# The first norm moved into the inputs' stage, with two queue and engine moves in the projection and the compressor

## The chip, the cores and the metric

The kernel runs on one core of one Trainium2 chip. A core has five engines that run side by side, each in its own program order: TensorE (PE, matrix products), VectorE (DVE), ScalarE (ACT), GpSimd (POOL) and SyncE (SP, which here only issues transfers). Semaphores tie them together; 16 DMA engines move data. The time is device microseconds (us) of one execution, the median of several.

## The reference

One step of a decoder layer in float32: 1024 prompt tokens and 8 x 4 sample tokens of width 1024. The input is normalised per token, scaled and shifted by two vectors of adaLN, and projected; beside attention over compressed, selected and window keys runs an S5 state-space branch; an MLP closes the layer. What the change touches:

```python
def rms_norm(x, g):
    y = x * lax.rsqrt(jnp.mean(x * x, axis=-1, keepdims=True) + RMS_EPS)
    return y * g

def mixer_inputs(x, c, lw):
    mods = ada_mods(c, lw['w_ada'], lw['b_ada'])          # silu(c) @ w_ada + b_ada, in 6 parts
    h = rms_norm(x, lw['g_norm_mix']) * (1 + mods[1]) + mods[0]
    proj = jnp.einsum('ntd,de->nte', h, lw['w_in'])
    ...

def compress(x, pe, w1, b1, w2):                          # cached keys and values, in chunks of 16 tokens
    ...
    part = jnp.einsum('ncsgd,jsde->jncge', x, w1c)
    hid = b1 + jnp.einsum('jsd,jsde->e', pec, w1c)
    for j in range(CMP_RATIO):
        hid = hid + part[j, :, j:j + n_cmp]
    return jnp.einsum('ncge,ef->ncgf', jax.nn.silu(hid), w2)
```

## The kernel before

The kernel is a row of stages: inputs, norm, SSM, projection, compressor, prompt attention, decode attention, tail. Each opens its own buffers and semaphores and closes with a barrier of all engines. Within a stage each engine has its own hand-written program.

**Inputs** (`stage_inputs`, L95). SP loads the nine blocks of rows of x (`xrow`: eight of 128 prompt tokens, one of 32 sample tokens), then the four blocks of adaLN weights (`wada`, two buffers: block i+2 waits until the products of block i are done), then `wu`, the SSM's columns of the input weights. PE turns each block of rows (L177) so that channels lie on partitions; DVE copies the even blocks from PSUM to `xT`, ACT the odd ones, two halves of four channel groups each (L129). Then PE makes the adaLN products (L86) block by block, DVE copies them, PE sums them per channel (L92), and DVE adds the bias: `mod`.

**Norm** (`stage_norm`, L221). SP stores `xT` to DRAM (`x_keep`, for the tail; L258). On `xT`, in three slices of 352 tokens by 8 channel groups, ACT squares (L282), PE sums over channels with a matrix of ones (L303), ACT takes the root, DVE inverts and multiplies, and ACT scales and shifts by `amp` and `mod` (L272) into `hT`. The sample tokens, which have their own vectors, get two more DVE operations per channel group.

**SSM** (`stage_ssm`, L378). PE begins with the products of `hT` and `wu` (L549); SP begins with the loads of the SSM's parameters, which PE turns after the first 16 products (L528). The buffers of this stage lie where `xT` was.

**Projection** (`stage_project`, L1066, with `table_steps`, L933). PE multiplies `hT` by the input weights, block after block of 128 columns (x = 0, 1, ...; two weight buffers, `w_raw`). SP issues each block's weights when the products of block x-2 are done, and all else in program order between them: at x == 3 it issues the store `bias_lines` (`store_line`: eight rows of 383, each written 128 times, to DRAM) and at x == 5 the copies of the two window caches from DRAM to DRAM. ACT rounds the weights (`weights_hi`, L1186) and copies PE's sums from PSUM (L1201 to L1207), in this order:

```python
                    ins.then_inc(kept, 1)
                    if s == 0 and 1 <= x < NX - 1:
                        weights_hi(x + 1)
                if x == 1:
                    t_near_bias(act)
```

**Compressor** (`stage_compress`, L1251). There are 18 units: i = 0 and 1 are the prompt's keys and values, the other 16 the keys and values of the eight sequences' caches. POOL gathers the pages of a unit by two indirect transfers of 128 x 2048 (`raw`, two buffers). They are then regrouped by key head into `byg`, one half by DVE (L1455), the other by ACT (L1400). PE turns a unit in eight turns of four transposes (L1336); ACT rounds each turn to `x_hi` (L1382), DVE makes the remainder `x_lo` (L1426), and PE multiplies: eight steps (sp) of three products. Unit i+1 is turned between the steps of unit i. The sums go to `hid` by DVE (L1433) and ACT (L1394); after step 6 PE makes the second products (L1313, L1319) of the unit before. The order of turns and steps on PE:

```python
                    if i + 1 < NI and NH[i + 1] == 2 and sp >= 1:
                        turn(i + 1, sp - 1)
                        if sp == 7:
                            turn(i + 1, sp)
                    if sp == 6 and i >= 1:
                        second(i - 1)
```

## Time and profile before

| | us |
|---|---|
| median of 3 runs | 2280.38 (2274.66 to 2280.99) |
| the profiled execution | 2283.11 |
| its span in the trace | 2281.1 |
| inputs, from 0 to | 47.62 |
| norm, to | 83.3 |
| SSM, to | 298.4 |
| projection, to | 467.5 |
| compressor, to | 681.8 |
| attention of prompt and decode, to | 1104 |
| tail, to | 2281.1 |

The trace has one row for each instruction or for a run of like ones: start, duration, engine, line, what is written and read; in brackets how long the engine had idled and what ended that. A name with a q (SPq) is the engine's sequencer, which issues transfers. PE is busy for 91% of the span, in the tail nearly throughout; the holes lie in the stages before it. Over the span the page gives PE's granted clock in 40 slices, mostly at 0.9 and over.

### The profile page before, as it was taken

The numbers are of one execution on the slowest core, as the hardware profiler recorded it, in microseconds if no ns is written. First come the engines' busy times: TensorE is split into PE (matmuls) and PEld (weight loads), VectorE is DVE, ScalarE is ACT, GpSimd is POOL, SyncE is SP. The second block draws the span as 40 slices with busy tenths as digits, with TensorE's granted clock in tenths as the row PEclk, the third lists the DMA queues.
The fourth block names the chain that finished last, engine by engine and source line by source line (L and its number), as shares of the span: only waits on it lengthen the run. The fifth ranks groups of instructions, "written<-read, shape, count | busy, mean of one in ns | idle before, by whom it ended". The sixth has DMA issues, their size and how long they took to land.

```text
span 2281.1 us, 33862 instructions
## 1 busy us (share of the span) xinstructions
PE 2069.8 (91%) x13956; PEld 1860.0 (82%) x13956; DVE 913.3 (40%) x1739; ACT 805.0 (35%) x1603; POOL 532.6 (23%) x478
## 2 busy tenths in 40 slices
PE   6694988969989999967799999999999999999997
PEld 4463678957775677745799999999999999999997
DVE  1568031126654777537411114454214313313424
ACT  2421321136654777734422223233113203302313
POOL 0190000011106656322122221121212222211220
PEclk8897889979996999979899999999999999999999
DMA  8102135354523321186611113111111111111111
GB/s 333 26 1 40 79 66 146 81 166 185 188 75 92 89 79 55 38 306 264 218 47 47 40 44 123 38 38 47 47 47 47 47 47 38 47 47 47 47 56 77
DMA packets 219065, 201.98 MB, mean 89 GB/s; under 512 B 37374, under 2 KB 202214, under 8 KB 210256
## 3 DMA queue, kind: packets, MB, share of 16 engines
q1 hardware_dynamic: 207118, 131.82, 19.9%
q0 software_dynamic: 9216, 67.11, 7.8%
q8 instruction: 111, 1.82, 0.3%
q10 hardware_dynamic: 2578, 0.88, 0.2%
q14 instruction: 42, 0.34, 0.0%
HBM read 178.05 MB, written 21.58 MB: 88 GB/s over the span
## 4 chain that ended last, share of the span: by engine, by line
PE 49%; DMA 1%; DVE 0%; ACT 0%; SPq 0%; issue 0%; ACTq 0%; DVEq 0%
PE ps L2286 16%; PE ps L2284 16%; PE ps L2285 16%; PE ps L2430 1%; DMA tail<-in_w_in 1%; DMA tail<-x_keep 1%; PE ps L2451 0%; DVE tail L2795 0%; ACT tail L2624 0%; DVE tail L2771 0%; SPq L2396 0%; SPq L2409 0%; ACT tail L2615 0%; DVE tail L2713 0%; ACT tail L2529 0%
## 5 line engine op out<-in xcount | busy, mean ns | idle before, releaser
L2284 PE MATMUL ps<-tail,tail 128*128 128x356 f32 (+2 forms) x2304 | 757.1, 329 | 12.0 <-POOL tail L2682 9.4
L2286 PE MATMUL ps<-tail,tail 128*128 128x356 f32 (+2 forms) x2304 | 750.7, 326 | 0.0
L2285 PE MATMUL ps<-tail,tail 128*128 128x356 f32 (+2 forms) x2304 | 748.7, 325 | 0.0
L2682 POOL TENSOR_TENSOR tail<-tail,tail 128x1024 fp32r<-128x1024 f32 x96 | 232.4, 2420 | 926.6 <-ACT tail L2529 926.6
L2284 PEld LDWEIGHTS ps<-tail,tail 128*128 128x128 f32 x2304 | 435.8, 189 | 15.1 <-POOL tail L2682 9.6
L2285 PEld LDWEIGHTS ps<-tail,tail 128*128 128x128 f32 x2304 | 435.8, 189 | 2.6 <-issue 0.2
L2286 PEld LDWEIGHTS ps<-tail,tail 128*128 128x128 f32 x2304 | 435.9, 189 | 0.0
L2529 ACT ACTIVATE tail<-tail 128x1024 fp32r<-128x1024 f32 x96 | 101.0, 1052 | 322.8 <-PE ps L2286 314.3
L2713 DVE SCALAR_TENSOR_TENSOR tail<-ps,mod,tail 128x346 f32<-128x346 f32 (+2 forms) x120 | 68.7, 572 | 345.8 <-PE ps L2286 336.4
L1746 POOL TENSOR_SCALAR pr<-pr,row_reciprocals,gT 128x640 f32<-128x640 f32 (+7 forms) x128 | 98.7, 781 | 112.8 <-DVE row_reciprocals L1865 111.2
L2584 ACT ACTIVATE tail<-tail,tail 128x346 f32<-128x346 f32 (+2 forms) x96 | 55.9, 583 | 195.5 <-DVE tail L2753 100.2
L1426 DVE TENSOR_TENSOR x_lo<-ps,x_hi 128x512 fp32r<-128x512 f32 (+1 forms) x136 | 89.0, 673 | 79.8 <-ACT x_hi L1382 78.7
L2696 DVE TENSOR_TENSOR tail<-tail,tail 128x346 f32<-128x346 f32 (+2 forms) x48 | 28.9, 601 | 210.0 <-ACT tail L2549 210.0
L2747 DVE TENSOR_TENSOR tail<-ps,tail 128x346 f32<-128x346 f32 (+2 forms) x96 | 50.3, 524 | 154.2 <-PE ps L2286 95.2
L1382 ACT ACTIVATE x_hi<-ps 128x512 fp32r<-128x512 f32 (+1 forms) x136 | 75.8, 580 | 79.0 <-PE ps L1336 78.7
L1657 PE MATMUL ps<-consts,pr 128*128 128x128 f32 (+7 forms) x592 | 93.5, 284 | 8.2 <-POOL pr L1746 6.4
L2284 PE MATMUL ps<-h_lo,w_hi 128*128 128x352 f32 x264 | 88.8, 336 | 9.2 <-DVE w_lo L1218 9.2
L1336 PE MATMUL ps<-consts,byg 128*128 128x128 f32 (+1 forms) x544 | 80.4, 279 | 18.4 <-DMA byg<-out 18.4
L1809 ACT ACTIVATE pr<-ps,nmax 128x640 f32<-128x640 f32 (+7 forms) x128 | 90.0, 703 | 19.1 <-DVE nmax L1845 16.3
L1336 PEld LDWEIGHTS ps<-consts,byg 128*128 128x128 f32 (+1 forms) x544 | 67.0, 147 | 33.2 <-DMA byg<-out 18.9
L1845 DVE TENSOR_REDUCE nmax<-ps 128x1 f32<-128x640 f32 (+7 forms) x128 | 90.6, 708 | 4.4
L2285 PE MATMUL ps<-h_hi,w_lo 128*128 128x352 f32 x264 | 88.0, 334 | 0.0
(481 smaller groups left out, 3024.2 us busy)
## 6 DMA issues: line engine op xcount, KB each, us to landing
tail<-in_w_ff SPq DMA_DIRECT2D x64, 512.0 KB
wada_late<-in_w_ada SPq DMA_DIRECT2D x32, 512.0 KB, 4.0
wada<-in_w_ada SPq DMA_DIRECT2D x4, 2048.0 KB, 12.2
tail<-in_w_in SPq DMA_DIRECT2D x16, 512.0 KB
x_keep<-xT SPq DMA_DIRECT2D x1, 4224.0 KB, 11.5
h_keep<-hT SPq DMA_DIRECT2D x1, 4224.0 KB
tail<-x_keep SPq DMA_DIRECT2D x1, 4224.0 KB, 13.1
xrow<-in_x_prompt SPq DMA_DIRECT2D x8, 512.0 KB, 8.2
```

What stands on the lines that cost most here:

```text
L1336: mm = pe.transpose(bank[y % 4][:, o:o + m], byg[0:m, i % 2, half, g, s:s + 2, :].rearrange("p s d -> p (s d)"), e.ident[0:m, 0:m])
L1382: act.activation(to, src, ACT.Copy).then_inc(hi_kept, 1)
L1426: dve.tensor_tensor(to, src, move(i, b, xhi)[1], ALU.subtract).then_inc(lo_kept, 1)
L1657: mm = pe.transpose(b[0:n, (t % 4) * P:(t % 4 + 1) * P], pr[:, u % NPR, t * n:(t + 1) * n], e.ident)
L1746: pool.tensor_scalar(p, p, rinv[:, k:k + 1], gT[:, qb, h:h + 1], ALU.mult, ALU.mult).then_inc(scaled, 1)
L1809: act.activation(p, score(s), ACT.Exp, bias=nmax[:, s % 4:s % 4 + 1], accum_out=rsum[:, sum_at(s):sum_at(s) + 1]).then_inc(exps_done, 1)
L1845: dve.tensor_reduce(nmax[:, u % 4:u % 4 + 1], s, AXX, ALU.max, negate=True).then_inc(maxima_done, 1)
L2284: pe.matmul(out, whi[:, kw, :], xlo(kx), start=(i == 0), stop=False)
L2285: pe.matmul(out, wlo[:, kw, :], xhi(kx), start=False, stop=False)
L2286: mm = pe.matmul(out, whi[:, kw, :], xhi(kx), start=False, stop=(i == n - 1))
L2529: act.activation(whi[:, x % 2], wraw[:, x % 2], ACT.Copy).then_inc(w_hi, 1)
L2682: pool.tensor_tensor(wlo[:, x % 2], wraw[:, x % 2], whi[:, x % 2], ALU.subtract).then_inc(w_split, 1)
```

## The change

Three stages are edited.

**Inputs and norm.** `stage_norm` is gone. In `stage_inputs` ACT squares the rows of x as they arrive, with the sum of each row taken in the same instruction (`ssq`), and takes the root of all nine columns at once; DVE inverts it (`rstd`). DVE copies all turned blocks to `xT`. The rows are then scaled in place by `rstd`, the odd blocks by ACT, the even ones by DVE, and PE turns the scaled rows a second time (`turn_scaled`), three blocks ahead of each of the weight blocks 1, 2 and 3. ACT copies the first halves of these turns to `hT`, DVE the second halves. When `mod` is there, `hT` is scaled and shifted in place: the prompt tokens of four channel groups by ACT, of four by DVE, and the sample tokens by two DVE instructions. SP issues the store of `x_keep` behind `wu`. It isn't waited for in this stage: in the SSM ACT waits for it ahead of its copies to `UT`, and DVE ahead of `Fre` and `Fim`; these three buffers are now allocated last.

**Projection.** `bias_lines` is issued by ACT at the end of x == 1, the window copies by ACT at the end of x == 5; SP issues neither.

**Compressor.** POOL regroups both halves, and issues the gathers of unit i+2 behind the regrouping of unit i. Ahead of its first gathers it waits for the prompt's rows. PE makes two turns after each odd step.

```diff
@@ stage_inputs
+            sp.wait_ge(x_kept, 2 * TB + 2)
+            sp.dma_start(e.x_keep, e.xT[:, :, :]).then_inc(e.x_stored, 16)
...
+            act.wait_ge(sums_set, 1)
+            for tb in range(TB + 1):
+                n = tokens(tb)
+                load_wait(act, x_loaded[tb], 1)
...
+                act.activation(junk[0:n, tb % TB, :], xrow[0:n, tb, :], ACT.Square, accum_out=ssq[0:n, tb:tb + 1]).then_inc(squared, 1)
...
+            act.activation(rstd[:, :], ssq[:, :], ACT.Sqrt, bias=e.eps, scale=1.0 / D).then_inc(root, 1)
+            act.wait_ge(rstd_set, 1)
             for tb in range(1, TB + 1, 2):
-                copy_x(act, tb)
+                act.wait_ge(x_turned, 2 * tb + 2)
+                act.activation(xrow[:, tb, :], xrow[:, tb, :], ACT.Copy, scale=rstd[:, tb:tb + 1]).then_inc(rows_act, 1)
+            for tb in range(TB + 1):
+                act.wait_ge(h_turned, 2 * tb + 1)
+                out, src = turned_to(e.hT, tb, 0)
+                act.activation(out, src, ACT.Copy).then_inc(h_kept[0], 1)
+            act.wait_ge(amp_set, 2)
+            act.wait_ge(h_kept[0], TB + 1)
+            for k in range(KD // 2):
+                act.activation(e.hT[:, k, 0:T], e.hT[:, k, 0:T], ACT.Identity, bias=e.mod[:, k, 0:1], scale=amp[:, k, 0:1]).then_inc(modulated, 1)
...
+            def turn_scaled(tb):
+                n = tokens(tb)
+                pe.wait_ge((rows_dve, rows_act)[tb % 2], tb // 2 + 1)
+                for h in range(2):
+                    if tb >= 2:
+                        pe.wait_ge(h_kept[h], tb - 1)
+                    else:
+                        pe.wait_ge(x_kept, 2 * TB + 2)
+                    for k in range(4):
...
+                    mm.then_inc(h_turned, 1)
+
             for i in range(NBLK):
+                if i:
+                    for tb in range(3 * (i - 1), 3 * i):
+                        turn_scaled(tb)
                 load_wait(pe, w_loaded[i % 2], i // 2 + 1)
...
+            for tb in range(TB + 1):
+                for h in range(2):
+                    dve.wait_ge(x_turned, 2 * tb + h + 1)
+                    dve.tensor_copy(*turned_to(e.xT, tb, h)).then_inc(x_kept, 1)
+            dve.wait_ge(root, 1)
+            dve.reciprocal(rstd[:, :], rstd[:, :]).then_inc(rstd_set, 1)
+            dve.wait_ge(rstd_set, 1)
             for tb in range(0, TB + 1, 2):
-                copy_x(dve, tb)
+                n = tokens(tb)
+                dve.tensor_scalar(xrow[0:n, tb, :], xrow[0:n, tb, :], rstd[0:n, tb:tb + 1], None, ALU.mult).then_inc(rows_dve, 1)
             for i in range(NBLK):
+                if i:
+                    for tb in range(3 * (i - 1), 3 * i):
+                        dve.wait_ge(h_turned, 2 * tb + 2)
+                        dve.tensor_copy(*turned_to(e.hT, tb, 1)).then_inc(h_kept[1], 1)
...
+            dve.tensor_scalar(amp[:, :, :], e.mod[:, KD:2 * KD, :], 1.0, None, ALU.add).then_inc(amp_set, 1)
...
+            for k in range(KD // 2, KD):
+                dve.tensor_scalar(e.hT[:, k, 0:T], e.hT[:, k, 0:T], amp[:, k, 0:1], e.mod[:, k, 0:1], ALU.mult, ALU.add).then_inc(modulated, 1)
...
+            dve.tensor_tensor(by_sequence, by_sequence, each(amp[:, :, 1:NC9]), ALU.mult).then_inc(samples, 1)
+            dve.wait_ge(samples, 1)
+            dve.tensor_tensor(by_sequence, by_sequence, each(e.mod[:, 0:KD, 1:NC9]), ALU.add).then_inc(samples, 1)
...
-def stage_norm(nc, e, tag, src, gain, shift=None, scale=None, dst=None, keep=None, store=False):
...
@@ stage_ssm
+            load_wait(act, e.x_stored, 1)
             for b in range(U_FIRST):
                 keep_turned(b)
...
+            load_wait(dve, e.x_stored, 1)
             for l, m in ((0, 4), (4, 4), (8, 1)):
...
@@ stage_project
-                if x == 3:
-                    t_store_line(sp)
...
-                if x == 5:
-                    for o, b in ((e.s_k_win, e.cache_k_win), (e.s_v_win, e.cache_v_win)):
...
                 if x == 1:
                     t_near_bias(act)
+                    t_store_line(act)
+                if x == 5:
+                    for o, b in ((e.s_k_win, e.cache_k_win), (e.s_v_win, e.cache_v_win)):
...
@@ stage_compress
+            for i in range(2):
+                load_wait(pool, prompt_rows_landed[i], 2)
+            gather(2)
+            gather(3)
+            for i in range(2, NI):
+                load_wait(pool, pages_landed[i % 2], 2 * (i // 2))
+                pool.wait_ge(turned, first[i - 1])
+                for half in range(2):
+                    dst, src = regrouping(i, half)
+                    pool.tensor_copy(dst, src).then_inc(regrouped, 1)
+                if i + 2 < NI:
+                    gather(i + 2)
...
-                    if i + 1 < NI and NH[i + 1] == 2 and sp >= 1:
+                    if i + 1 < NI and NH[i + 1] == 2 and sp % 2 == 1:
                         turn(i + 1, sp - 1)
-                        if sp == 7:
-                            turn(i + 1, sp)
+                        turn(i + 1, sp)
```

Where instructions stand: PE in the inputs' stage, before. The rows with `xrow` are the turns, those with `wada` the adaLN products (eight to a block), those with `modrow` their sums:

```order
L177 MATMUL ps<-consts,xrow 128x128 x64
L177 MATMUL ps<-consts,xrow 128x32 x8
L86 MATMUL ps<-wada,scT 32x512 x16
L92 MATMUL ps<-consts,modrow 128x9 x4
L86 MATMUL ps<-wada,scT 32x512 x8
L92 MATMUL ps<-consts,modrow 128x9 x4
L86 MATMUL ps<-wada,scT 32x512 x8
L92 MATMUL ps<-consts,modrow 128x9 x8
```

The same engine and stage in the changed kernel:

```order
L204 MATMUL ps<-consts,xrow 128x128 x64
L204 MATMUL ps<-consts,xrow 128x32 x8
L86 MATMUL ps<-wada,scT 32x512 x8
L227 MATMUL ps<-consts,xrow 128x128 x24
L86 MATMUL ps<-wada,scT 32x512 x8
L92 MATMUL ps<-consts,modrow 128x9 x4
L227 MATMUL ps<-consts,xrow 128x128 x24
L86 MATMUL ps<-wada,scT 32x512 x8
L92 MATMUL ps<-consts,modrow 128x9 x4
L227 MATMUL ps<-consts,xrow 128x128 x16
L227 MATMUL ps<-consts,xrow 128x32 x8
L86 MATMUL ps<-wada,scT 32x512 x8
```

The second turns (L227) stand in threes of blocks ahead of the weight blocks 1, 2 and 3.

SP in the projection, before, from the store at x == 3 on (`out<-rows` stores the new key and value rows):

```order
L969 DMA bias_lines<-line 8x128x383
L1113 DMA w_raw<-in_w_in 128x8x128
L1123 DMA out<-rows 128x8x128
L1125 DMA out<-rows 32x128
L1113 DMA w_raw<-in_w_in 128x8x128
L1123 DMA out<-rows 128x8x128
L1125 DMA out<-rows 32x128
L1131 DMA out<-in_cache_k_win 8x4x16256
L1131 DMA out<-in_cache_v_win 8x4x16256
L1110 DMA w_raw<-in_w_in 128x8x64 x2
```

The same place in the changed kernel:

```order
L1032 DMA w_raw<-in_w_in 128x8x128 x3
L1040 DMA out<-rows 128x8x128
L1042 DMA out<-rows 32x128
L1032 DMA w_raw<-in_w_in 128x8x128
L1040 DMA out<-rows 128x8x128
L1042 DMA out<-rows 32x128
L1029 DMA w_raw<-in_w_in 128x8x64 x2
```

`bias_lines` and the window copies have left this queue; the weights follow each other with only the row stores between.

ACT in the compressor, one unit before:

```order
L1382 ACTIVATE x_hi<-ps 128x4x128 x4
L1400 ACTIVATE byg<-raw 128x16x2x64
L1394 ACTIVATE hid<-hid,cbias 64x2x255
L1382 ACTIVATE x_hi<-ps 128x4x128 x4
L1389 ACTIVATE low<-ps 64x512
```

One unit and the next one's first rows in the changed kernel:

```order
L1310 ACTIVATE x_hi<-ps 128x4x128 x4
L1322 ACTIVATE hid<-hid,cbias 64x2x255
L1310 ACTIVATE x_hi<-ps 128x4x128 x4
L1317 ACTIVATE low<-ps 64x512
L1310 ACTIVATE x_hi<-ps 128x4x128 x4
```

The regrouping that stood ahead of `hid` is gone from ACT (and likewise from DVE); on POOL two of them stand between the gathers.

## Rows read from the trace of the kernel before

**Rows 1.** Norm, projection, compressor: length, each engine's busy time (instructions), PE clock, DMA.

```profile
47.60:83.30 35.70, 16.33 (x48) 9.83 (x48) 21.46 (x45) 29.18 (x60) 0.00 (x0) 0.74 0.29 122
298.40:467.50 169.10, 152.60 (x950) 149.66 (x950) 33.61 (x41) 33.50 (x49) 5.77 (x18) 0.92 0.41 99
467.50:681.80 214.30, 179.66 (x1080) 148.46 (x1080) 125.76 (x192) 126.86 (x190) 32.05 (x32) 0.92 0.46 162
```

**Rows 2.** Timeline of inputs and norm, PE and SP: start, duration, instruction, [idle before].

```profile
9.93 9.73 PE L177 MATMUL ps<-consts,xrow 128*128 128x128 f32 x72
...
27.03 3.19 PE L86 MATMUL ps<-wada,scT 128*32 128x512 f32 x16 [4.09 <-DMA wada<-in_w_ada]
...
32.01 1.92 PE L86 MATMUL ps<-wada,scT 128*32 128x512 f32 x16 [0.42 <-DMA wada<-in_w_ada]
...
39.19 3.64 PE L86 MATMUL ps<-wada,scT 128*32 128x512 f32 x16 [4.27 <-DMA wada<-in_w_ada]
...
47.62 0.35 SPq L258 DMA_DIRECT2D x_keep<-xT  x1
...
83.36 9.91 PE L549 MATMUL ps<-wu,hT 128*128 128x512 f32 x16 [18.38 <-PEq L66]
```

**Rows 3.** Groups by line, forms apart: count, busy us, mean ns, idle before.

```profile
L2615 ACT ACTIVATE tail<-tail,tail 128x1024 f32<-128x1024 f32 x4 | 4.5, 1147 | 0.7 <-DVE tail L2782 0.7
...
L2788 DVE TENSOR_SCALAR tail<-tail,tail 128x1024 f32<-128x1024 f32 x4 | 2.9, 751 | 0.1
...
L129 DVE COPY xT<-ps 128x512 f32<-128x512 f32 x8 | 5.2, 687 | 3.6 <-PE ps L177 3.6
```

**Rows 4.** DMA issues on the page: count, KB, us from issue to landing.

```profile
x_keep<-xT SPq DMA_DIRECT2D x1, 4224.0 KB, 11.5
```

**Rows 5.** Timeline of the projection, SP's issues and ACT.

```profile
333.73 0.31 SPq L969 DMA_DIRECT2D bias_lines<-line  x1
351.88 0.38 SPq L1113 DMA_DIRECT2D w_raw<-in_w_in  x1
...
357.31 0.46 ACT L1207 ACTIVATE turn_in<-ps 128x352 f32<-128x352 f32 x1 [4.96 <-PE ps L2286]
369.69 1.06 ACT L1186 ACTIVATE w_hi<-w_raw 128x1024 fp32r<-128x1024 f32 x1 [11.91 <-DMA w_raw<-in_w_in]
...
378.23 0.46 ACT L1207 ACTIVATE turn_in<-ps 128x352 f32<-128x352 f32 x1 [6.78 <-PE ps L2286]
...
391.44 0.47 ACT L1207 ACTIVATE turn_in<-ps 128x352 f32<-128x352 f32 x1 [5.04 <-PE ps L2286]
```

**Rows 6.** Timeline of the compressor: a second product of PE, DVE's last sums.

```profile
558.92 1.10 PE L1319 MATMUL ps<-w2c,hid 64*128 64x64 f32 x8 [0.84 <-ACT hid L1394]
...
640.08 0.67 DVE L1433 TENSOR_TENSOR hid<-ps,low 64x510 f32<-64x510 f32 x1
...
651.27 0.67 DVE L1433 TENSOR_TENSOR hid<-ps,low 64x510 f32<-64x510 f32 x1
...
662.02 0.67 DVE L1433 TENSOR_TENSOR hid<-ps,low 64x510 f32<-64x510 f32 x1
...
672.28 0.67 DVE L1433 TENSOR_TENSOR hid<-ps,low 64x510 f32<-64x510 f32 x1
```

**Rows 7.** Timeline of the compressor's start, PE's turns.

```profile
488.02 0.69 PE L1336 MATMUL ps<-consts,byg 64*128 64x64 f32 x4 [7.59 <-DMA byg<-out]
...
496.24 1.08 PE L1336 MATMUL ps<-consts,byg 128*128 128x128 f32 x4
```

**Rows 8.** POOL: two groups by line, then two rows of the SSM's timeline.

```profile
L1148 POOL COPY vslc<-rows 128x512 f32<-128x512 f32 x2 | 1.2, 614 | 54.1 <-DVE rows L1245 54.1
...
L2682 POOL TENSOR_TENSOR tail<-tail,tail 128x1024 fp32r<-128x1024 f32 x96 | 232.4, 2420 | 926.6 <-ACT tail L2529 926.6
...
141.03 1.17 POOL L517 TENSOR_TENSOR w<-w 128x16 f32<-128x16 f32 x1
...
150.72 0.21 POOL L517 TENSOR_TENSOR w<-w 128x16 f32<-128x16 f32 x1
```

214 lines of the change are left out of this document (43 added, 171 removed).

## The prediction

> **What bounds the kernel now.** I read the stretches of the three stages that the change touches first, then each stage's timeline. In the norm stage PE works 16.33 of 35.70 us, in the projection 152.60 of 169.10, in the compressor 179.66 of 214.30 [rows 1]. So the first stage is a chain of the other engines that PE waits behind, and the other two are PE's, with holes. The stages are divided by barriers and the three edits lie in different ones, so the sum of their gains is the gain of the whole; later stages keep their work. The profiled execution took 2283.11 us and the median is 2280.38: I make the sum against the first and take 2.7 off at the end.
>
> **Part A: the norm goes into the inputs.** Removed: everything from the norm's first instruction at 47.62 to the SSM's first products at 83.36 [rows 2], 35.7 us with its barrier. What takes its place is paid in three pieces.
>
> First, the chain of the ada products. It ends with the fourth weight block, whose products start at 39.19, on landing; 8.43 us later the next stage begins [rows 2]. Block 3's load needs the buffer of block 1, whose products start at 27.03 [rows 2]. Now the turns of the scaled rows of tokens 0 to 2 stand ahead of these products on PE. When can they run? PE turned the nine blocks of x in 9.73 us from 9.93 [rows 2]; of the 18 copies DVE now does all, 16 of them of 0.69 us [rows 3] and two small ones. 16 x 0.69 + about 0.8 after the first half block (10.5) is 22.4. ACT's squares and root run beside that. Then DVE's reciprocal of nine columns, which I put at half a copy, and the scaling of the rows: DVE has blocks 0 and 2, ACT block 1 beside it, at 0.75 and 1.15 each (rows of such operations on 128x1024) [rows 3], so the third is there near 24.5. Three blocks of turns at PE's pace of 1.1 per block and the copies that free their banks are some 4 us: PE is free for the products near 28.5 instead of 27.03, so block 3's weights come about 1 us later (0 to 3). The products and the column sums behind it may gain something: the same 16 products took 1.92 us at 32.01 and 3.64 at 39.19, after a wait of 4.27 [rows 2], and now PE turns rows in part of that wait. 1.7 us for them is the upper end; I take half, 0.9, against the 1 us of delay. So mod is there where it was, near 47.
>
> Second, the modulation, now at the end of the stage: two small operations of DVE (together less than one 0.69 copy; I put 0.6), then ACT's four of 128x1024 at 1.15, 4.6 us; DVE's four at 0.75 and the two for the sample tokens, each at most a copy's 0.69, lie beside them, 4.4 [rows 3]. With the barrier that is in the 8.43 already, the SSM starts near 47.6 + 5.2 = 52.8 instead of 83.36: 30.5 saved.
>
> Third, x_keep. Its transfer took 11.5 us from issue [rows 4] and lay under the norm; now it is issued when DVE's copies are done, but behind wu on SP, and moves among the last weights and the SSM's parameters. The parameters are needed when the SSM's first products end, 9.91 us after its start [rows 2]. The two new waits for x_keep, of ACT ahead of UT and of DVE ahead of Fre and Fim, hold up all that these engines have queued behind them, and through them PE; but they stand later in the SSM than the parameters, and the transfer is issued in the stage before. I take 0.5 for both; if the whole 11.5 fell behind the SSM's start, the parameters would be about 3 us late, so 0 to 3. **A: 30 us saved**, 26 to 34.
>
> **Part B: the projection's queue.** SP issues bias_lines at 333.73. The weights of the fifth block of columns are issued at 351.88, and ACT waits 11.91 us for them until 369.69 [rows 5]. Behind that wait stand ACT's copies of PE's sums, so PE stops: the blocks' first copies stand at 357.31, 378.23 and 391.44, 20.92 us apart and then 13.21 [rows 5]. The excess is 7.7. With the store on ACT's queue (issued behind t_near_bias) these weights no longer stand behind it in one queue; ACT's own time for an issue is that of SP's row, 0.31, three times in the stage. The window copies go the same way; before, they cost no such gap (the spacing after them is the ordinary 13.21). They now move some two blocks of columns later, under other weight loads; that costs 0 to 3 by the same kind of wait, and I take 0.5. **B: 7 us**, 2 to 9.
> What speaks against it: the Trainium skill, "DMA: Bandwidth & Descriptors", section "Issuing engines are not separate DMA queues", says that transfers of several engines run on the same 16 DMA engines and that issuing from another one saves only the issue time. By that rule B would be near nothing and the time 7 us longer; the stage's mean DMA share of 0.41 [rows 1] leaves room for both transfers, so I give it the smaller chance (a rival below).
>
> **Part C: the compressor.** Three things change. (1) The regrouping of a unit leaves ACT and DVE. The last units before show its price: hid of the last three comes 640.08, 651.27, 662.02, 672.28; the unit of 11.19 us has a regrouping and eight second products, that of 10.26 the same products and no regrouping [rows 6]. The turns of PE are the same in both, so regrouping costs 0.93 per unit; PE's wait of 0.84 for hid at its second products [rows 6] is where it falls. 15 units by 0.93 are 14 us. (2) Turning in pairs leaves PE the same turns and products, only grouped; and puts the fourth turn, after which ACT makes hid, one step earlier. I take 0; it could cost a few tenths per unit (5 us) or nothing. (3) POOL's unit is now two copies of 128x2048 and two gathers. A gather is 32.05 / 32 = 1.0 us [rows 1]. A copy: from below four times the 614 ns of a 128x512 copy, 2.5 us; from above twice the 2420 ns of the 128x1024 operation with two inputs, 4.8 [rows 8]. I take 2.5, the same operation: 2 x 2.5 + 2 x 1.0 = 7.0, under 10.26, so it is hidden, with two buffers in which to be late. By the upper end it would be 11.7, and not hidden.
> (4) The start. PE's second unit of prompt rows waited 7.59 us for its transfer until 488.02, since the first four gathers moved beside it, and the first gathered unit is turned at 496.24 [rows 7]. Now POOL gathers after the prompt rows. By the shapes these are 1.0 MB of rows and 4.2 MB of gathers, which together took from 467.5 to 488.0, 20.5 us. The rows alone are a fifth, but in short pieces: I put 10 us, 477.5. The first unit's gathers, 2.1 MB at that pace, take 8.3 more, and POOL's two copies 5, which now stand in the path: 491, so 5 us earlier (0 to 9). **C: 19 us**, 8 to 25.
>
> **Sum:** 30 + 7 + 19 = 56. 2283.1 - 56 = 2227; less 2.7, **2224 us**.
>
> **Rivals.**
> (a) B gives nothing: the weights wait as long for shared transfers as for the queue. 2224 + 7 = 2231. For it: bias_lines is slow (from 333.73 to past 351.88); against it: the later weights come in time though other stores move beside them. 0.12.
> (b) A gives 8 us less: the rows' scaling and the second turns push the weight blocks back, or x_keep holds up the SSM's parameters by its whole 11.5 us. 2224 + 8 = 2232. For it: every step of A but one hangs on another engine's. 0.12.
> (c) POOL's copies go at the upper end: a unit of 11.7 us sets the compressor's beat instead of 10.97, the mean of the last two kinds of unit with regrouping (11.19 and 10.75 [rows 6]). 15 x 0.73 = 11 us lost, 5 of the start gained: C is -6. 2283.1 - 37 + 6 - 2.7 = 2249. 0.10.
> (d) Slower than before: POOL stands still while DVE works. POOL's operation of 128x16 took 1.17 us at 141.03 and 0.21 at 150.72 [rows 8]: something holds it for the length of others' operations. In the compressor DVE is busy 125.76 us [rows 1], 7.9 per unit of 16, 6.7 without the regrouping. If both add up at the copies' upper end, a unit is 11.7 + 6.7 = 18.4: 15 x 7.4 = 111 lost, 2224 + 19 + 111 - 5 = 2349. It decides from a unit of 10.97 + 42 / 15 = 13.8 us.
> The Trainium skill, "SBUF — State Buffer", section "Who interferes with whom", says that DVE holds GpSimd's reads while it runs an instruction with two SBUF inputs, and not with one. By that rule (d) does not come: DVE's operations in the compressor read one input from PSUM, and those in the row at 141.03 two from SBUF. The row agrees, no run before shows the other half. 0.04 for (d).
>
> **Chances and range.** Forecast 0.62, (a) 0.12, (b) 0.12, (c) 0.10, (d) 0.04. Range: upward to (c) with its neighbours, 2250; downward the three upper ends would give 2212, and I take 2206, since two or three steps of A may each come out better. Faster by over 0.3% (6.8 us, about what a measurement here can tell from none): the first four, 0.95; within 0.3%: 0.02, the mild half of (d); slower 0.03.
>
> **What would show each step.** A: the SSM's first products near 53 and its parameters' turns some 10 us behind; wrong if ACT's or PE's idle time ahead of the last ada products grows over 3 us, or if the first u products are followed by a wait for a DMA. B: no wait over 2 us of ACT for w_raw, and first copies 13.2 apart. C: PE without waits for hid, units of about 10.0, POOL's copies near 2.5 us; wrong if PE waits for byg from POOL. The whole is wrong first if POOL's copies pass 4 us, or if fewer holes let the clock fall somewhere else.

## The result and the profile after

The changed kernel took 2264.18 us (median of 11 runs, 2251.22 to 2270.89) against 2282.07 of the kernel before in the same series: a ratio of 0.9908, interval 0.9889 to 0.9927. It is faster by 18 us; 56 were forecast, and the time lies above the forecast's range. The profiled execution took 2264.32 us, its span is 2262.5.

By stage (us, from the first instruction of one stage to that of the next; the span of each kernel's profiled execution):

| | before | after | gain | forecast |
|---|---|---|---|---|
| inputs and norm | 83.3 | 50.3 | 33.0 | 30 |
| SSM | 215.1 | 230.0 | -14.9 | 0 |
| projection | 169.1 | 189.3 | -20.2 | 7 |
| compressor | 214.3 | 194.2 | 20.1 | 19 |
| attention and tail | 1599.3 | 1598.7 | 0.6 | 0 |
| span | 2281.1 | 2262.5 | 18.6 | 56 |

The norm's move and the compressor's edits came out as forecast. The 37 us that are missing were lost in two stages: in the SSM, where nothing but the place of three buffers and two waits was edited, and in the projection. The stretches of SSM, projection and compressor after the change (columns as in [rows 1]):

```profile
50.30:280.30 230.00, 183.44 (x1218) 133.76 (x1218) 98.67 (x133) 48.87 (x86) 68.49 (x78) 0.78 0.14 40
280.30:469.60 189.30, 158.32 (x950) 155.39 (x950) 33.51 (x41) 33.50 (x49) 5.77 (x18) 0.87 0.37 88
469.60:663.80 194.20, 178.98 (x1080) 148.85 (x1080) 104.65 (x176) 96.40 (x174) 90.33 (x64) 0.92 0.52 179
```

In the projection PE's busy time went from 152.60 to 158.32 with the same 950 records, and the stage grew by 20: most of it is standstill, the rest a lower clock (0.87 for 0.92). In the compressor it is the other way round: the busy time is nearly that of [rows 1], and of 34.6 us of standstill 15.2 are left.

Inputs and the start of the SSM, PE and ACT:

```profile
10.54 11.55 PE L204 MATMUL ps<-consts,xrow 128*128 128x128 f32 x72
...
29.25 1.92 PE L86 MATMUL ps<-wada,scT 128*32 128x512 f32 x16
...
40.01 1.92 PE L86 MATMUL ps<-wada,scT 128*32 128x512 f32 x16
...
44.77 4.63 ACT L179 ACTIVATE hT<-hT,mod,amp 128x1024 f32<-128x1024 f32 x4 [4.62 <-DVE amp L277]
...
50.38 8.93 PE L466 MATMUL ps<-wu,hT 128*128 128x512 f32 x16 [6.56 <-PEq L66]
...
60.58 0.44 PE L451 MATMUL ps<-consts,finrow 128*128 128x128 f32 x2 [0.81 <-DMA finrow<-in_state_ssm_im]
```

Block 1's products start at 29.25 instead of 27.03 and the last block's at 40.01 instead of 39.19 [rows 2]: the chain of weight blocks is 0.8 us later. The last products take 1.92 us instead of 3.64, with no wait ahead of them, since the second turns fill it, and the column sums behind them 1.95 instead of 3.58. The modulation on ACT is 4.63 us, and the SSM's products start 33 us earlier. The transfer of `x_keep`, 11.5 us from issue before [rows 4], took 23.9 among its new neighbours; PE's whole wait for the SSM's parameters is 0.81.

What the SSM lost is lost in one phase, its output products, which start behind a wait of PE of some 20 us for DVE's scan and run until the sample tokens' products. First the changed kernel, then the kernel before:

```profile
192.65:230.37 37.72, 37.72 (x211) 30.33 (x211) 0.84 (x2) 3.70 (x7) 0.00 (x0) 0.50 0.33 136
```

```profile
224.96:249.30 24.34, 24.34 (x212) 19.74 (x211) 0.84 (x2) 3.50 (x7) 0.00 (x0) 0.85 0.51 211
```

The same products, PE busy throughout in both: at a clock of 0.50 (1.2 GHz) for all of 37.72 us after, at 0.85 on average before (0.50 at the start, 1.00 later on). That is 13.4 of the 14.9 us.

The projection after, ACT with its own issues, and SP's issue of the weights of x = 7:

```profile
321.12 0.32 ACTq L888 DMA_DIRECT2D bias_lines<-line  x1
...
355.66 1.06 ACT L1099 ACTIVATE w_hi<-w_raw 128x1024 fp32r<-128x1024 f32 x1 [14.21 <-DMA w_raw<-in_w_in]
...
386.55 0.81 ACTq L1129 DMA_DIRECT2D out<-in_cache_k_win  x1
...
392.04 0.46 ACT L1114 ACTIVATE qT<-ps 128x352 f32<-128x352 f32 x1 [5.04 <-PE ps L2198]
409.99 1.06 ACT L1099 ACTIVATE w_hi<-w_raw 128x1024 fp32r<-128x1024 f32 x1 [17.48 <-DMA w_raw<-in_w_in]
...
418.47 0.47 ACT L1114 ACTIVATE qT<-ps 128x352 f32<-128x352 f32 x1 [6.73 <-PE ps L2198]
```

```profile
386.53 1.00 SPq L1029 DMA_DIRECT2D w_raw<-in_w_in  x2
```

The wait for the weights of x = 4 is still there, 14.21 us instead of the 11.91 of [rows 5]. A second one of 17.48 has come: the weights of x = 7 were issued at 386.53 in the same microsecond as the window copies and landed 23.5 us later. Both follow from one event: SP issues these weights when the products of block 5 are done, and ACT issues the copies behind its last sums of block 5. The first copies of the blocks on either side stand at 392.04 and 418.47, 26.4 us apart where 13.2 is the ordinary spacing.

The compressor after: PE's first turn of a gathered unit, DVE's first and last full sums, POOL's regrouping in a middle unit; then the group of all regroupings:

```profile
492.72 1.97 PE L1265 MATMUL ps<-consts,byg 128*128 128x128 f32 x8 [5.35 <-POOL byg L1229]
...
513.05 0.67 DVE L1353 TENSOR_TENSOR hid<-ps,low 64x510 f32<-64x510 f32 x1
...
561.69 3.73 POOL L1229 COPY byg<-raw 128x2048 f32<-128x2048 f32 x2 [3.64 <-PE ps L1265]
...
654.33 0.67 DVE L1353 TENSOR_TENSOR hid<-ps,low 64x510 f32<-64x510 f32 x1
```

```profile
L1229 POOL COPY byg<-raw 128x2048 f32<-128x2048 f32 x32 | 59.7, 1892 | 57.3 <-PE ps L1265 50.5 <-DMA raw<-in_cache_k_cmp,rowidx 6.8
```

From 513.05 to 654.33 are 14 units, 10.09 each. The same sums before:

```profile
519.63 0.67 DVE L1433 TENSOR_TENSOR hid<-ps,low 64x510 f32<-64x510 f32 x1
```

From there to 672.28 [rows 6] are 152.65 us, 10.90 each: 11.4 us gained in the units. The two stretches, before and after (columns as in [rows 1]), show that PE's work in them is the same and that its 10.9 us of standstill have gone:

```profile
519.63:672.28 152.65, 141.72 (x869) 116.11 (x868) 102.45 (x154) 102.46 (x153) 20.59 (x22) 1.00 0.44 163
```

```profile
513.05:654.33 141.28, 141.28 (x869) 116.42 (x868) 85.02 (x141) 77.51 (x140) 67.92 (x48) 1.00 0.47 171
```

The other 8.7 us are the start: the first full sum comes 43.4 us into the stage instead of 52.1. A copy on POOL takes 1.89 us, and POOL waits 3.64 us for PE in a unit, not the other way round.

### The profile page after: what moved, and what is told of

It reads as the page before. It is cut to its first block, busy times and chain, and to the rows that moved or that the text cites. A ratio compares the mean times of both kernels' runs of the same rounds, so it can differ in the third digit from the quotient of the medians.

```text
span 2262.5 us, 33825 instructions
## 1 busy us (share of the span) xinstructions
PE 2076.7 (92%) x13980; PEld 1873.6 (83%) x13980; DVE 889.4 (39%) x1709; ACT 766.3 (34%) x1556; POOL 590.5 (26%) x511
## 4 chain that ended last, share of the span: by engine, by line
PE 50%; DMA 1%; DVE 0%; ACT 0%; POOL 0%; issue 0%; SPq 0%; ACTq 0%; DVEq 0%
PE ps L2198 16%; PE ps L2196 16%; PE ps L2197 16%; PE ps L2342 1%; DMA tail<-x_keep 1%; PE ps L2363 0%; DMA tail<-in_w_br_ssm 0%; POOL tail L2594 0%; DVE tail L2683 0%; SPq L2308 0%; ACT tail L2527 0%; DVE tail L2625 0%; ACT tail L2441 0%; ACTq L2223 0%; ACT tail L2471 0%
## 5 line engine op out<-in xcount | busy, mean ns | idle before, releaser
L2196 PEld LDWEIGHTS ps<-tail,tail 128*128 128x128 f32 x2304 | 435.4, 189 | 12.6 <-POOL tail L2594 9.7
L2198 PE MATMUL ps<-h_hi,w_hi 128*128 128x352 f32 x264 | 90.0, 341 | 0.0
L1569 PEld LDWEIGHTS ps<-consts,pr 128*128 128x128 f32 (+7 forms) x592 | 68.4, 140 | 20.7 <-POOL pr L1658 9.8
## 6 DMA issues: line engine op xcount, KB each, us to landing
x_keep<-xT SPq DMA_DIRECT2D x1, 4224.0 KB, 23.9
```

The costliest lines, as they stand in the source:

```text
L1569: mm = pe.transpose(b[0:n, (t % 4) * P:(t % 4 + 1) * P], pr[:, u % NPR, t * n:(t + 1) * n], e.ident)
L2196: pe.matmul(out, whi[:, kw, :], xlo(kx), start=(i == 0), stop=False)
L2198: mm = pe.matmul(out, whi[:, kw, :], xhi(kx), start=False, stop=(i == n - 1))
```

## The experiments

All times in us. "Output" is the phase of the SSM's output products in the profile with its mean clock, the rest are stage lengths in the profile.

| kernel | median (lowest to highest) | ratio to before, interval | SSM | output, clock | projection | compressor |
|---|---|---|---|---|---|---|
| after | 2264.2 (2251.2 to 2270.9) | 0.9908, 0.9889 to 0.9927 | 230.0 | 37.7, 0.50 | 189.3 | 194.2 |
| e1_both_stores_back | 2232.9 (2230.0 to 2242.6) | 0.9809, 0.9785 to 0.9833 | 214.3 | 22.7, 0.92 | 169.3 | 193.9 |
| e2_windows_back | 2238.9 (2234.8 to 2252.7) | 0.9824, 0.9801 to 0.9846 | 229.8 | 37.7, 0.50 | 176.3 | 194.3 |
| e3_bias_back | 2254.2 (2243.5 to 2261.4) | 0.9874, 0.9846 to 0.9902 | 228.2 | 37.7, 0.50 | 184.4 | 194.0 |
| e4_compressor_only | 2260.5 (2258.2 to 2264.2) | 0.9915, 0.9899 to 0.9930 | 214.8 | 22.8, 0.91 | 169.3 | 194.1 |
| e5_split_and_windows_early | 2225.4 (2222.8 to 2241.7) | 0.9752, 0.9728 to 0.9776 | 230.3 | 37.7, 0.50 | 164.6 | 193.5 |
| e6_windows_early | one run, 2234.2 | | 214.7 | 22.8, 0.91 | 169.4 | 194.4 |
| e7_products_in_the_wait | 2232.3 (2229.1 to 2234.6) | 0.9773, 0.9756 to 0.9791 | 213.7 | 21.0, 1.00 | 168.8 | 194.2 |
| e8_pool_single_turns | one run, 2246.8 | | 230.1 | 37.7, 0.50 | 169.8 | 193.4 |
| e9_pairs_alone | one run, 2240.3 | | 214.5 | 22.6, 0.92 | 169.0 | 205.2 |
| e10_all_together | 2228.4 (2227.2 to 2243.5) | 0.9777, 0.9753 to 0.9801 | 230.1 | 37.7, 0.50 | 162.9 | 194.2 |
| e11_changed_with_products | 2255.4 (2243.8 to 2262.8) | 0.9885, 0.9860 to 0.9909 | 214.4 | 22.7, 0.92 | 189.6 | 194.2 |
| e12_before_with_products | 2283.1 (2278.7 to 2287.3) | 1.0006, 0.9996 to 1.0017 | 215.1 | 24.3, 0.85 | 169.2 | 214.0 |
| e13_all_with_22_products | 2228.8 (2224.7 to 2239.5) | 0.9782, 0.9759 to 0.9804 | 216.3 | 21.1, 1.00 | 163.0 | 194.0 |
| e14_changed_with_22_products | 2249.4 (2245.4 to 2253.5) | 0.9873, 0.9857 to 0.9888 | 215.2 | 21.0, 1.00 | 185.3 | 193.9 |
| e15_before_with_22_products | 2279.3 (2277.2 to 2294.7) | 1.0006, 0.9990 to 1.0022 | 226.9 | 37.1, 0.51 | 171.3 | 213.2 |
| e16_four_in_the_phase | 2229.5 (2228.0 to 2230.8) | 0.9772, 0.9755 to 0.9788 | 220.9 | 29.9, 0.81 | 164.1 | 193.9 |
| e17_eight_in_the_phase | 2231.1 (2229.4 to 2238.3) | 0.9788, 0.9768 to 0.9808 | 221.3 | 29.7, 0.94 | 163.0 | 193.9 |
| e18_22_ahead_and_four_in | 2228.6 (2223.6 to 2233.6) | 0.9770, 0.9748 to 0.9791 | 217.6 | 24.7, 1.00 | 162.8 | 193.9 |

Where the runs of a kernel lie in two groups, the profiled executions with an output phase of 37 us lie in the upper one (after, e2, e3, e5, e10, e15) and those with 21 to 23 us in the lower (e1, e13). The other runs have no profile. Their mean clock over the span goes with the group (after: 0.935 to 0.939 in the upper, 0.942 to 0.944 in the lower), so they are put down to this phase by their time and clock.

**e1: the projection's two transfers back on SP.**

```diff
+                if x == 3:
+                    t_store_line(sp)
...
+                if x == 5:
+                    for o, b in ((e.s_k_win, e.cache_k_win), (e.s_v_win, e.cache_v_win)):
+                        sp.dma_start(...)
...
-                    t_store_line(act)
-                if x == 5:
-                    for o, b in ...: act.dma_start(...)
```

> The changed kernel with both transfers of the projection back on SP: bias_lines at x == 3, the window copies at x == 5. The projection took 169.1 us before and 189.3 after the change. Theory Q (moving the transfers cost the whole difference): projection 169 us, the total near 2244 us (2264 less 20), and ACT waits near 11.9 us for x = 4's weights as before. Rival S (the projection is longer for what the earlier stages left in the queues or the clock): the projection stays over 180. On the clock in the SSM's output products (0.50 for 37 us in the profile of the changed kernel, 8 us before): if the change brings it, this profile has it too; if it is a draw of each execution, some of these profiles will and some won't.

Measured: 2232.9, projection 169.3. The whole of the projection's loss is the two moved transfers. The total fell by more than the 20 us, because this profile and three of its five runs have the SSM's output phase short, and the median of the changed kernel has it long.

**e2 and e3: one transfer back at a time.** The diffs are the two halves of e1's.

> The changed kernel with the window copies alone back on SP at x == 5; bias_lines stays on ACT. Theory W (the copies now run beside x = 7's weights, for which ACT waited 17.48 us): that wait goes, projection near 171 to 175 us, total near 2248. Rival L (bias_lines on ACT's queue is what costs, its wait of 14.21 us for x = 4's weights was 11.91 before): the projection stays above 185 and the total within 4 us of the changed kernel's.

> The changed kernel with bias_lines alone back on SP at x == 3; the window copies stay on ACT at x == 5. Theory W: the wait of 17 us for x = 7's weights stays, projection near 187 to 190 us, total 2262 to 2266. Rival L: projection near 172, total near 2247. If the queue of bias_lines matters for x = 4's weights as I forecast, ACT's wait for them is longer here than in e2_windows_back.

Measured: projection 176.3 with the windows back, 184.4 with bias_lines back, 169.3 with both. So the window copies on ACT cost 15.1 us (e3 less e1) and bias_lines on ACT 7.0 (e2 less e1). Each figure comes from one profile, and the same projection code took 189.3, 189.6 (e11) and 185.3 (e14); but the lower groups of run times give nearly the same steps (means of 2231.5 in e1, 2237.8 in e2, 2245.8 in e3 and 2252.0 after: 6.2, 14.3 and 20.5 us above e1). Theory W holds for the larger part, with both stages a little outside its ranges, and half of rival L with it: bias_lines on ACT's queue isn't neutral, it costs as much as it was forecast to gain. The rows say why. e1, SP's issues and ACT's wait:

```profile
301.11 0.30 SPq L888 DMA_DIRECT2D bias_lines<-line  x1
320.84 0.37 SPq L1032 DMA_DIRECT2D w_raw<-in_w_in  x1
```

```profile
337.08 1.06 ACT L1105 ACTIVATE w_hi<-w_raw 128x1024 fp32r<-128x1024 f32 x1 [10.36 <-DMA w_raw<-in_w_in]
```

e2, ACT's issue and its wait:

```profile
320.25 0.31 ACTq L888 DMA_DIRECT2D bias_lines<-line  x1
...
355.48 1.06 ACT L1103 ACTIVATE w_hi<-w_raw 128x1024 fp32r<-128x1024 f32 x1 [16.36 <-DMA w_raw<-in_w_in]
```

e3, ACT's issue of the windows and its wait:

```profile
379.15 0.82 ACTq L1130 DMA_DIRECT2D out<-in_cache_k_win  x1
...
402.62 1.06 ACT L1101 ACTIVATE w_hi<-w_raw 128x1024 fp32r<-128x1024 f32 x1 [17.52 <-DMA w_raw<-in_w_in]
```

From the issue of bias_lines to the landing of the weights of x = 4 are 36.0 us before [rows 5], 36.0 in e1, 35.9 in e3, 35.2 in e2 and 34.5 after, on whichever queue. The weights are issued 13 to 20 us behind the store. The trace has no landing for the store itself, but until then it is alone, and its pace can be read (e1, the last three columns are clock, DMA share and GB/s):

```profile
304.00:320.00 16.00, 16.00 (x80) 15.94 (x80) 1.42 (x2) 2.16 (x4) 0.00 (x0) 0.74 0.44 49
```

At 49 GB/s its 1532 KB take 32 us; by this estimate it ends near 334. The weights land at 337.08, so by it they land when the store has ended. On ACT the store is issued later against PE's blocks (40.6 us into the stage in e2, 35.3 in e1), and the weights come 13.0 us behind it (e2) instead of 19.7 (e1), so less of it has passed. The windows do the same: in e3 and after, weights issued beside them land 23.5 us later.

**e4: the compressor's change alone on the kernel before.**

> The kernel before with the compressor of the changed kernel and nothing else. The compressor took 214.3 us before and 194.2 after. Theory: the gain of 20 us stands by itself: total near 2262, compressor 194 us. Rival (the compressor is shorter because the stages ahead end otherwise): under 12 us. Inputs, norm and SSM are those of before: if the long slow clock in the SSM's output products is a draw of each execution, the times of single runs spread over some 13 us here as well; if the change brings it, they lie within some 3 us.

Measured: 2260.5, compressor 194.1: its gain stands by itself. Its six runs lie within 6 us. The 76 runs of the kernel before, in all series, lie from 2273 to 2288 (one of 9233 apart) without a gap as wide as that between the two groups of kernels with the new front. So the two groups were seen with the new front and not with the new compressor alone.

**e5 and e6: smaller pieces, and the windows where the DMA engines stand idle.** e6 moves the window copies into the SSM, behind the loads of its parameters; e5 also cuts the store:

```diff
-        sp.dma_start(rb.rearrange("p h w -> h p w"), line[:, None, :].to_broadcast([HQ, P, BW])).then_inc(lines_stored, 16)
+        sp.dma_start(rb.rearrange("p h w -> h p w")[:, 32 * piece:32 * piece + 32, :],
+                     line[:, None, :].to_broadcast([HQ, 32, BW])).then_inc(lines_stored, 16)
...
-                if x == 3:
-                    t_store_line(sp)
+                if 3 <= x <= 6:
+                    t_store_line(sp, x - 3)
```

> Both stores on SP as in e1_both_stores_back, with two further changes: bias_lines is stored in four pieces of 32 of its 128 repeats, one behind the weights of x = 3, 4, 5 and 6 each, and the window copies are issued in the SSM behind the loads of its parameters, where the DMA engines stand idle. In five profiles the weights of x = 4 landed 34.5 to 36.0 us after the issue of bias_lines, on either queue. Theory E (a load issued while a large store is under way lands when that store ends; what counts is how much of the store is left, not its queue): a piece takes some 9 us, no weights wait over 3 us for it, blocks 13.2 us apart throughout, projection 161 to 163 us against 169.3 in e1_both_stores_back, the total some 7 us under it. Rival R (the weights wait for something else at x = 4, such as the store of the new rows): projection 168 to 170.

> e1_both_stores_back with the window copies issued in the SSM and bias_lines whole at x == 3. Theory E: ACT's wait for the weights of x = 6 (4.19 us in e1_both_stores_back) goes, PE gains nothing by it since it was covered: projection 168.5 to 169.5; the SSM keeps its length but for the clock. Rival: the 4 MB disturb the SSM's loads, and the SSM grows by over 3 us.

Measured: e6 as expected, projection 169.4, SSM 214.7. In e5 the wait is gone:

```profile
314.64 0.30 SPq L891 DMA_DIRECT2D bias_lines<-line  x1
334.36 0.37 SPq L1035 DMA_DIRECT2D w_raw<-in_w_in  x1
334.78 0.49 SPq L891 DMA_DIRECT2D bias_lines<-line  x1
```

```profile
340.16 1.05 ACT L1104 ACTIVATE w_hi<-w_raw 128x1024 fp32r<-128x1024 f32 x1
353.36 1.05 ACT L1104 ACTIVATE w_hi<-w_raw 128x1024 fp32r<-128x1024 f32 x1
```

ACT doesn't wait for weights at x = 4 any more, and the blocks follow 13.2 us apart. The first piece has gone when they are issued: from 324 on the DMA engines stand idle.

```profile
324.00:334.00 10.00, 10.00 (x59) 10.00 (x58) 1.23 (x1) 1.88 (x3) 0.00 (x0) 0.92 0.00 0
```

Theory E holds. The projection is 164.6, outside the 161 to 163 expected, and 162.8 to 164.1 in the later kernels with the same store: 4.7 to 6.5 us gained, somewhat under the 7 expected. e5 has the lowest median of all, 2225.4, 2.5% under the kernel before; the intervals of e7, e10, e13, e16, e17 and e18 overlap with its own.

**e8 and e9: the compressor's two edits apart.** e8 has POOL's regrouping with the turns in the order of before, e9 the turns in pairs with everything else in the compressor as in the kernel before; both have the new front.

> e1_both_stores_back with the compressor's turns one after each step as before (two at step 7), the regrouping on POOL as in the changed kernel. The compressor takes 194 us there and 214.3 before. Theory: POOL's regrouping and the later gathers bring all of it, and the order of turns nothing: 193 to 197 us. Rival (the pairs, which put the fourth turn and with it hid one step earlier, take the wait of 0.84 us per unit away by themselves): over 202.

> e1_both_stores_back with the compressor of before, in which only the order of turns is changed to pairs: DVE and ACT regroup, POOL gathers at once. Without pairs (e8_pool_single_turns) POOL's compressor took 193.4 us, with them 193.9. If the pairs bring hid early enough to end PE's wait for it (0.84 us in each of 15 units), the compressor takes about 202; if the regrouping on ACT and DVE holds the units in any order, 212 to 216.

Measured: e8 193.4, so beside POOL's regrouping the pairs bring nothing. e9 205.2: alone they bring 9.1 of the 20 us. PE's waits in the compressor of e9, then its waits for `hid` in the kernel before (us in total, times, longest):

```profile
PE ps L1255 <- DMA byg<-out: 17.6, 2, 10.4
PE ps L1232 <- ACT hid L1312: 3.6, 8, 2.5
PE ps L1238 <- ACT hid L1312: 3.1, 7, 2.1
```

```profile
PE ps L1313 <- ACT hid L1394: 8.6, 8, 2.7
PE ps L1319 <- ACT hid L1394: 7.7, 8, 2.2
```

Both edits shorten the same wait for `hid`, each by itself: of the 16.3 us before, the pairs alone leave 6.7, POOL's regrouping alone 3.1 (e8), both together 2.5 (after). The first row, the wait of the start, is 18.4 us before and 17.6 in e9, so the pairs don't touch it; with POOL's later gathers it is 12.6 (7.3 for the prompt rows and 5.3 for POOL).

**e7, e10 to e12: products in the wait ahead of the output phase.** 18 products of 128x512 of constants, read by nothing, behind the SSM's sample inputs:

```diff
             mm.then_inc(S["sample_inputs_done"], 1)
+            for _ in range(18):
+                pe.matmul(bank[5][:, :], ident, e.consts[:, 0:512], start=True, stop=True)
```

> e1_both_stores_back with 18 products of 128x512 more, of constants, into a PSUM bank that is free and written over later, in the 20 us in which PE waits ahead of the SSM's output products; nothing reads them. In profiles of kernels with the new front these output products ran at a clock of 0.50 for 37.7 us (three of four) or took 22.7 (one), and single runs of one kernel lie in two groups 11 to 14 us apart; with the front of before they took 24.3 and 22.8, and the six runs of e4_compressor_only spread over 6 us. Theory K (the phase starts at the low level because PE has stood still ahead of it, and stays there in some executions): with PE at work until the start it runs at 1.00, 19 to 20 us, in every execution; the runs form one group, spread under 6 us, near 2228. Rival (the level in this phase does not depend on what PE did ahead of it): two groups as before, the upper one near 2243, and the profile may show 0.50 again.

> e5_split_and_windows_early (bias_lines in four pieces on SP, window copies in the SSM) with the 18 products in PE's wait ahead of the SSM's output products (nothing reads them). Theories E and K together: one group of runs, 2222 to 2228; SSM near 213.5, projection 161 to 165. If the two groups of runs had another cause, some runs lie near 2240.

> The changed kernel as it is, with the 18 products in PE's wait ahead of the SSM's output products (nothing reads them). Its eleven runs lay at 2251 to 2253 (four) and 2262 to 2271 (seven). Theory K: all runs in one group, 2247 to 2254, so 12 to 16 us of the changed kernel's median are the clock's. Rival: two groups.

> The kernel before with the same 18 products at the same place (nothing reads them). Its output products took 24.3 us in the profile, some 8 us of it at the low level. Theory K: 21 us, the SSM 3 us shorter, the median 2 to 5 us under that of before. If the products only did something for the changed kernel's clock, no change within 2 us.

Measured: e7 gave one group, 2229 to 2235, and the phase at 1.00. e10 and e11 did not: two of five runs at 2242 and over, and 2244 to 2263. e7's and e10's rows:

```profile
173.12 18.23 PE L547 MATMUL ps<-consts 128*128 128x512 f32 x36
193.41 0.28 PE L551 MATMUL ps<-consts,Sre 128*16 128x128 f32 x1 [2.06 <-DVE xs L842]
```

```profile
171.58 15.72 PE L550 MATMUL ps<-consts 128*128 128x512 f32 x36
192.64 0.39 PE L554 MATMUL ps<-consts,Sre 128*16 128x128 f32 x1 [5.34 <-DVE xs L845]
```

In e10 the 18 products ran faster and left 5.34 us of standstill, and the phase began at the low level; in e7 2.06 were left. So theory K was only half tested, which e13 to e15 mend with 22 products. e12 brought nothing, with 24.3 us in the phase behind the same 5.34 us.

**e13 to e15: 22 products.**

> e10_all_together with 22 products in PE's wait instead of 18 (nothing reads them). In e7_products_in_the_wait the 18 took 18.23 us, PE then waited 2.06 us and the SSM's output products ran at 1.00; in e10_all_together and e11_changed_with_products they took 15.72, PE waited 5.34, and the output products began at 0.50. Theory K, sharpened (the wait left over ahead of the output products decides: 5.3 us puts PE at the low level, 2.1 doesn't): 22 take 19.2 us, under 2 us are left, all runs in one group at 2222 to 2228, output products 20 to 21.5 us at 1.00. Rival (the level there is a draw that the wait doesn't bear on): two groups again, the upper near 2242.

> The changed kernel with 22 such products. Its runs with 18 spread from 2243.8 to 2262.8, without any from 2251.2 to 2270.9. Theory K: the upper part goes, 2243 to 2253 (the projection's waits still vary), SSM 212 to 214 us. Rival: spread of 18 us as before.

> The kernel before with 22 such products. With 18 its output products still took 24.3 us behind a wait of 5.34, and the median was that of before. Theory K: 20 to 21.5 us, the SSM 3 us shorter, the median 2 to 5 us under that of before; with e14 that gives what the folded norm is worth where both kernels run this phase at the full level. Rival: no change.

Measured: in e13 and e14 the phase ran at 1.00 in the profile, and eight of nine runs lie in the lower group; but one of e13 is at 2239.5. e15 refutes theory K. Three of twelve runs of the kernel before, with 22 products, lie at 2292.8 to 2294.7, the others at 2277.2 to 2280.6, and its profile is one of the three:

```profile
201.24 19.15 PE L630 MATMUL ps<-consts 128*128 128x512 f32 x44
222.29 0.28 PE L634 MATMUL ps<-consts,Sre 128*16 128x128 f32 x1 [1.91 <-DVE xs L923]
```

```profile
225.00:250.00 25.00, 25.00 (x133) 20.06 (x132) 0.00 (x0) 2.26 (x5) 0.00 (x0) 0.50 0.43 179
```

PE was at the full level until 1.91 us ahead of the phase, its first transpose took 0.28 us as at the full level, and then the phase fell to 0.50 and stayed there. The long phase also comes with the old norm stage: it isn't a property of the folded norm's arithmetic, and the standstill ahead doesn't decide alone. With the old norm stage it was seen with the 22 products alone: without them no run of the kernel before (9233 apart) lies above 2288.2.

**e16 to e18: larger products within the phase.** Four or eight products of 128x512 of constants among the sixteen groups of output products of e5, read by nothing; e18 has 22 ahead as well.

```diff
+                    if (4 * b + q // 2) % 4 == 3:
+                        pe.matmul(bank[3][:, :], ident, e.consts[:, 0:512], start=True, stop=True)
```

> e5_split_and_windows_early with four products of 128x512 of constants among the SSM's output products, one behind each of their four blocks, into a free bank (nothing reads them); none ahead of them. In the kernel before with 22 products ahead the output products began at the full level and still fell to 0.50, and in e13 one run of five lay 11 to 15 us above the others: the wait ahead doesn't decide alone. Theory M (the output products, small and each with its own weights, don't by themselves bring the level up in every execution, and larger products among them do): one group, 2224 to 2231, the phase 21 to 28 us with the four products (0.9 to 1.8 us each). Rival D (a draw that nothing in the phase bears on): about two runs of six at 2238 to 2246, as in e5.

> The same with eight such products, one behind every second of the sixteen groups. Theory M: one group, 3 to 5 us above that of e16, 2227 to 2235, the phase never at 0.50 throughout. Rival D: two groups 14 us apart, both higher by the products' time.

> e13_all_with_22_products with four products in the phase as in e16. Theory M: begun at the full level it stays there in all executions: one group, 2225 to 2232, the phase 24 to 25 us. Rival D: one run in five at 2240 or over, as in e13.

Measured: e16 one group, within 2.8 us, where e5 had spread over 19. The phase of e16 took 29.9 us, over the 28 expected, and e17's median lies 1.6 us above that of e16, not 3 to 5. In e16 the clock rises inside the phase, 11 us behind its start (us 201 to 209):

```profile
201.00:205.00 4.00, 4.00 (x23) 2.50 (x21) 0.00 (x0) 1.09 (x2) 0.00 (x0) 0.65 0.94 406
205.00:209.00 4.00, 4.00 (x37) 3.28 (x38) 0.00 (x0) 0.12 (x1) 0.00 (x0) 1.00 0.34 144
```

The first of the larger products in e16, then in e17 (two records each):

```profile
201.78 2.07 PE L574 MATMUL ps<-consts 128*128 128x512 f32 x2
```

```profile
194.34 1.12 PE L574 MATMUL ps<-consts 128*128 128x512 f32 x2
```

In e16 it ran at the low level, and the clock rose as it ended. In e17 it took the 1.1 us of the full level, so there the clock had risen before any of the eight, and e18's phase began at the full level: only one profile shows the rise beside a larger product.

In e17 four runs lie within 3 us and one 6 us above them, in e18 all within 10. No run of the fifteen shows the 14 us, against about one in three of e5, e10 and e13 together (five of sixteen). That speaks for theory M: these output products alone leave the level open, and a few larger ones among them may close it. It isn't a proof. By a chance of one in three, fifteen runs without the long phase would come about twice in a thousand; but e16 to e18 ran on another chip than e5, e10 and e13, a rival that no run excludes, and what selects the long phase in one execution stays open. It was also no gain in the mean: e16's products cost what the missing upper group saves (2229.5 against e5's mean of 2229.6).

## Why the prediction was wrong, and where it was right

**Part A, the stage.** Right: 33.0 us saved at the SSM's start for 30.5. The chain of weight blocks came 0.8 us later where 1 was taken, the last products ran at 1.92 us and gave the whole 1.7 where half was taken, and the sums behind them gave 1.6 more. The wait for parameters cost 0.8 for the 0.5 taken. x_keep's transfer doubled, to 23.9 us, and no cost beyond that 0.8 shows: without the output phase e1's SSM is 191.6 us long, against 190.8 before.

**Part A, what follows.** The step that failed is "later stages keep their work": they kept it, but not its clock. In the profiled execution the SSM gave back 14.9 us, 13.4 of them in its output phase. In kernels with the new front and no products added there 17 of 37 runs lie in an upper group, 11 to 16 us above the other; in the changed kernel it is 7 of 11, so its median has it. The profile before showed this phase at 0.85 with its first stretch at 0.50, and I had not read that as a price that could grow; "the clock fall somewhere else" stands among the signs of being wrong, without a rival or a price. Nothing in the experiments shows how the new front raises the share of such executions, so this cause stays open; e15 shows that the old norm stage, with 22 products ahead of the phase, can have them too.

**Part B.** Wrong in its premise, and the largest miss: 27 us between forecast and result. "These weights no longer stand behind it in one queue" took the queue for the cause of the wait. The weights land at the end of the store on either queue (34.5 to 36.0 us from its issue, five kernels). The mean DMA share of 0.41, which I read as room for both transfers, said nothing of this: the store alone shows 0.44 for 16 us (e1), and the small load beside it still waited for its end. The rule of the Trainium skill that I had set against it ("DMA: Bandwidth & Descriptors", section "Issuing engines are not separate DMA queues"), to which I gave 0.12, is what the runs bear out, and they go beyond it: the move not only saves nothing, it costs 7.0 us, because ACT's place in the program is later than SP's (5.3 us later in the stage, e2 against e1). For the window copies I bounded the cost of "some two blocks of columns later" at 3 us. It was 15.1, for the same reason. The kernel before, SP and then ACT:

```profile
370.92 0.81 SPq L1131 DMA_DIRECT2D out<-in_cache_k_win  x1
...
385.92 1.01 SPq L1110 DMA_DIRECT2D w_raw<-in_w_in  x2
```

```profile
396.93 1.06 ACT L1186 ACTIVATE w_hi<-w_raw 128x1024 fp32r<-128x1024 f32 x1 [5.02 <-DMA w_raw<-in_w_in]
```

There the copies were issued 15.0 us ahead of the next weights, which landed 11.0 us behind their own issue, and PE didn't feel ACT's wait of 5.02. Now the whole 23.5 us lie behind the weights' issue. That the copies "cost no such gap" before was a matter of their place, and I let them be moved for nearly nothing. Rival (a) named the mechanism, and put its price at nothing gained rather than at a loss.

**Part C.** Right in sum, 20.1 for 19, with two errors that cancel: the units gave 11.4 us (0.81 in each of 14) where 14 were worked out, and the start 8.7 where 5 were. A POOL copy takes 1.89 us, under the lower bound of 2.5 from a smaller copy; rivals (c) and (d) fall with it, though DVE is at work in 6.1 of each 10.1 us. "The pairs bring nothing" holds beside POOL's regrouping and not by itself (e9): the pairs end most of the same wait, so the two gains don't add.

**The sum.** 33.0 - 14.9 - 20.2 + 20.1 + 0.6 = 18.6. Without the two moves in the projection the same change gives 2232.9 (e1), 0.9809 of before. That lies inside the range of 2206 to 2250, 9 us above the forecast; part of it is luck, since three of e1's five runs have the short output phase. The range's upper end held no case in which an edit that was forecast as a gain turns into a loss of 20 us.

## What to carry to other kernels

A transfer moved to another engine's queue kept its cost here for the loads around it; ask when it is issued against the next load that someone waits for, how long it lasts, and whether it can be cut or put where the DMA engines stand idle (e5: a store of some 32 us in four pieces, 4 MB into a stage with a mean DMA share of 0.14). When two edits cure the same wait, their gains don't add. And a stretch in which PE is busy at a clock of 0.50 to 0.85 is a price that can grow in other executions of the same code, here from 22.7 to 37.7 us: read the clock of each stretch before counting it as fixed.

## What the hardware showed that I had not expected

- Weights of 512 KB, some 4 us from issue to landing alone, landed 34.5 to 36.0 us behind the issue of a store of 1.5 MB, or 23.4 to 26.0 behind that of copies of 4 MB. The large transfer was issued up to 20 us ahead or in the same microsecond, from the same queue or another.
- PE busy without a gap for 37.7 us on small products, each with its own weights, stayed at 1.2 GHz in some executions (after, e2, e3, e5, e8, e10). In others the clock rose to 2.4 GHz 3.6 us (e11) or 7.4 us (before) behind the start. In one it fell from the full level in the phase's first microsecond and stayed low (e15). With four products of 512 columns among them it rose in the one profile (e16), and no run of five took the longer time.
- POOL copied 128x2048 in 1.89 us, beside a DVE that was at work in 85.02 of 141.28 us; ACT took 1.91 for the same copy in the kernel before.
